# Expert weight tiles laid out and loaded in pairs, one 1 MB transfer for two ring slots

## The reference, cut to what matters

```python
q = jnp.einsum('td,de->te', xt, w_query).reshape(n_tok, PEER_HEADS, 2, HALF_KEY)
sc = jnp.einsum('thpk,hpnk->thpn', q, sub_keys)
va, ia = lax.top_k(sc[:, :, 0], PEER_TOPK)
vb, ib = lax.top_k(sc[:, :, 1], PEER_TOPK)
...
gate = jax.nn.softmax(top, axis=-1)
...
act = _gelu(jnp.einsum('tkd,td->tk', w_down[eb], xb))
return jnp.einsum('tk,tkd->td', gb * act, w_up[eb])
```

## Time and profile before

| | us |
|---|---|
| median of 3 runs | 1558.21 |
| runs | 1556.63, 1558.33, 1558.21 |
| span of the profiled execution (its own time is not printed beside it) | 1555.7 |
| TensorE busy | 1539.2 (99%) |
| VectorE, GpSimd, ScalarE busy | 1129.0, 742.5, 640.0 |
| down stage (first to last of lines 1307 to 1309) | 439.7 to 1021 |
| up stage (lines 1669 to 1671) | 1021.5 to 1544 |

### The profile page before, as it was taken

One profiled execution on the slowest core, in us unless ns is written; L12 is line 12 of the kernel. 1 busy time (PEld: TensorE's weight loads), 2 busy tenths in 40 slices (PEclk: granted clock), 3 DMA queues, 4 the chain that ended last, 5 costly groups with the idle time before them and its releaser, 6 DMA issues.

```text
span 1555.7 us, 23483 instructions
## 1 busy us (share of the span) xinstructions
PE 1539.2 (99%) x8604; PEld 1388.1 (89%) x8604; DVE 1129.0 (73%) x2355; ACT 640.0 (41%) x851; POOL 742.5 (48%) x452
## 2 busy tenths in 40 slices
PE   8999999999999999999999999999999999999997
PEld 8888899888899999999999999988888888888885
DVE  5564262477999877687759763788888888888796
ACT  5323244423234456446644663343333333333333
POOL 1543572224346976777678767732222322323230
PEclk9999999999999999999999999999999999999998
DMA  8532250332245987899799879999999999999991
GB/s 308 188 108 82 95 176 28 108 136 96 81 142 185 352 273 249 318 416 330 244 348 416 303 252 342 375 358 351 346 349 341 354 341 345 346 350 350 372 350 58
DMA packets 141147, 410.84 MB, mean 264 GB/s; under 512 B 15344, under 2 KB 49392, under 8 KB 140528
## 3 DMA queue, kind: packets, MB, share of 16 engines
q1 hardware_dynamic: 97984, 253.86, 46.6%
q0 software_dynamic: 36864, 134.23, 23.3%
q10 hardware_dynamic: 6192, 21.32, 3.5%
HBM read 363.22 MB, written 46.14 MB: 263 GB/s over the span
## 4 chain that ended last, share of the span: by engine, by line
PE 89%; DVE 9%; issue 1%; DMA 0%; POOL 0%; DVEq 0%; SPq 0%; ACT 0%
PE ps L1670 11%; PE ps L1671 11%; PE ps L1669 11%; PE ps L1307 10%; PE ps L1309 10%; PE ps L1308 10%; PE ps L433 6%; PE ps L435 6%; PE ps L434 6%; PE ps L1640 1%; PE ps L1642 1%; DVE gmat L1007 1%; DVE gmat L1000 1%; DVE gmat L1001 1%; DVE gmat L997 1%
## 5 line engine op out<-in xcount | busy, mean ns | idle before, releaser
L1525 ACT ACTIVATE w_hi<-raw 128x1024 fp32r<-128x1024 f32 x252 | 266.6, 1058 | 339.5 <-PE ps L1671 302.9
L1307 PE MATMUL ps<-b_hi,w_hi 128*128 128x384 f32 x1024 | 346.5, 338 | 0.2 <-POOL w_lo L1491 0.2
L1309 PE MATMUL ps<-b_hi,w_lo 128*128 128x384 f32 x1024 | 342.4, 334 | 0.0
L1308 PE MATMUL ps<-b_lo,w_hi 128*128 128x384 f32 x1024 | 342.2, 334 | 0.0
L1491 POOL TENSOR_TENSOR w_lo<-raw,w_hi 128x1024 fp32r<-128x1024 f32 x119 | 286.7, 2410 | 107.6 <-ACT w_hi L1525 106.3
L1499 POOL DMA_INDIRECT rows<-in_w_up,expert x128 | 151.7, 1185 | 341.4 <-DVE ps L1738 329.4
L1671 PE MATMUL ps<-w_hi,b_lo 128*128 128x512 f32 x768 | 298.8, 389 | 0.0
L1670 PE MATMUL ps<-w_lo,b_hi 128*128 128x512 f32 x768 | 298.8, 389 | 0.0
L1669 PE MATMUL ps<-w_hi,b_hi 128*128 128x512 f32 x768 | 298.8, 389 | 0.0
L1704 DVE SCALAR_TENSOR_TENSOR rows<-rows,ps 128x1024 f32<-128x1024 f32 x128 | 155.6, 1219 | 92.8 <-DMA rows<-in_w_down,expert 85.4
L1745 DVE TENSOR_TENSOR w_lo<-raw,w_hi 128x1024 fp32r<-128x1024 f32 x133 | 162.8, 1224 | 69.4 <-ACT w_hi L1525 69.4
(11 more groups left out here) (265 smaller groups left out, 2481.5 us busy)
## 6 DMA issues: line engine op xcount, KB each, us to landing
raw<-in_down_t SPq DMA_DIRECT2D x128, 512.0 KB
raw<-in_up_t SPq DMA_DIRECT2D x128, 512.0 KB
raw<-in_units SPq DMA_DIRECT2D x75, 512.0 KB, 3.4
act_d<-act_t SPq DMA_DIRECT2D x128, 192.0 KB
c<-act_d SPq DMA_DIRECT2D x128, 192.0 KB
gate_d<-gmat ACTq DMA_DIRECT2D x32, 512.0 KB
v<-gate_d SPq DMA_DIRECT2D x16, 512.0 KB
i<-gate_d SPq DMA_DIRECT2D x16, 512.0 KB
```

The source lines that it names most:

```text
L1307: nc.tensor.matmul(out, ring.w_hi[:, s, w], b_hi[:, c, 0:DT], start=c == 0, stop=False)
L1308: nc.tensor.matmul(out, ring.w_hi[:, s, w], b_lo[:, c, 0:DT], start=False, stop=False)
L1309: last = nc.tensor.matmul(out, ring.w_lo[:, s, w], b_hi[:, c, 0:DT], start=False, stop=c == KC - 1)
L1525: nc.scalar.activation(w_hi[:, u % W4, :], raw[:, u % W4, :], ACT.Copy).then_inc(hi_done, 1)
```

## The change

Both weight arrays are laid out so that two consecutive tiles lie side by side in a partition's row of 8 KB. SP loads such a pair with one transfer of 1 MB into two neighbouring slots of the ring. The pair is issued at the odd tiles, once both slots are free. A single semaphore, that of the even slot, tells that a pair has landed. The first eight tiles are still loaded one by one, now as halves of the 8 KB rows.

```diff
-            def load(u):
-                sp.wait_ge(split_done, u - W4 + 1)
-                src = t["down_t"][u] if u < TILES else t["up_t"][u - TILES]
-                sp.dma_start(raw[:, u % W4, :], src).then_inc(raw_full[u % W4], 16)
+            def load_pair(u):
+                s = u % W4
+                sp.wait_ge(split_done, u - W4 + 2)
+                src = t["down_t"][u // 2] if u < TILES else t["up_t"][(u - TILES) // 2]
+                sp.dma_start(raw[:, s:s + 2, :].rearrange("p a n -> p (a n)"), src).then_inc(raw_full[s], 16)
...
                 sp.dma_start(t["act_d"][u], act_t[:, u % ACTS, :]).then_inc(act_stored[u % ACTS], 16)
-                load(u + 2 * W4)
+                if u % 2:
+                    load_pair(u + 2 * W4 - 1)
...
             for j in range(TILES - 2 * W4):
-                load(TILES + j + 2 * W4)
+                if j % 2:
+                    load_pair(TILES + j + 2 * W4 - 1)
                 load_act(j + 2 * W4)
...
             def high_part(u):
-                act.wait_ge(raw_full[u % W4], 16 * (u // W4) + 16)
+                act.wait_ge(raw_full[u % W4 if u < 2 * W4 else u % W4 // 2 * 2], 16 * (u // W4) + 16)
...
-            ("front", ins["units"]), ("query", ins["units"][FRONT_UNITS:]), ("down", ins["down_t"]))]
+            ("front", ins["units"]), ("query", ins["units"][FRONT_UNITS:]),
+            ("down", [ins["down_t"][u // 2, :, u % 2 * D:(u % 2 + 1) * D] for u in range(2 * RING)]))]
...
-        "down_t": c(w_down[0].reshape(NK, NK, KC, P).transpose(1, 3, 2, 0)).reshape(NK, P, D),
-        "up_t": c(w_up[0].reshape(NK, NK, D).transpose(1, 0, 2)),
+        "down_t": c(w_down[0].reshape(NK, NK // 2, 2, KC, P).transpose(1, 4, 2, 3, 0)).reshape(NK // 2, P, 2 * D),
+        "up_t": c(w_up[0].reshape(NK, NK // 2, 2, D).transpose(1, 0, 2, 3)).reshape(NK // 2, P, 2 * D),
```

## The result

The changed kernel takes 1567.21 us (1566.08 to 1569.1, four runs) against 1557.42 us (1556.37 to 1558.33) for the one before on the same chip: 1.0064 times as long, with an interval of 1.0052 to 1.0076, or 9.8 us. The forecast was 4.1 us, and the top of its range is passed by 0.2 us. The profiled execution has a span of 1564.9 us against 1555.7, so 9.2 us of the difference are in the trace. In the file after the change the lines lie one to three further down: the pair's load is L1436, the high part L1528, the Gelu L1534, the gate copy L1545, GpSimd's low part L1494.

The account below looks back on a forecast made before the run. The prediction took TensorE, busy 1539.2 of 1555.7 us, to set the time; 0 + 2.3 + 1.8 = 4.1 us of stalls on the median 1558.2 gave 1562.3 us, range 1556.5 to 1567.

Parts of the forecast that it names:

- the removed issues: SP's queue: 124 of 248 weight loads go, 0.33 us each, on a queue that mostly waits; gain 0.
- a queue already full: First gate stores: loads of tiles 56 and 57 took 16.5 and 16.2 us, read as a backlogged DMA queue.
- the hidden case: Rival: pairs land soon enough everywhere, for instance if 8 KB pieces drain the queue faster; 1558.2 us, chance 0.38.
- The two terms of the stores: TensorE stalls in the first and second gate-store stretches of the down stage: 2.3 us and 1.8 us.
- the turn ahead of tile 89: Second gate stores: TensorE's turn of VectorE's picks, up to 2.6 us late if gathers slow down.
- The first gathers: Tiles 18 and 19: pair has 7.0 us to land, expected between 4.9 and 8.9, middle 6.9; cost 0.
- three places: Down-stage places priced: first gathers 0, first gate stores 2.3, second gate stores 1.8 us.
- The layout: First eight tiles as halves of 8 KB rows, same 4 KB pieces at another pitch: cost 0.
- faster: Rival: TensorE is fed at another rate, with only 4.9 us of waits open; about 1554 us, chance 0.06.
- The gathers or stores paying: Rival: weights win DMA share, so gate stores or gathers come late; about 1561 us, chance 0.12.
- The loop: Rival, up stage: pairs over 10.5 us lengthen rounds; at 11.5 us, 1.0 us in each of 30, 1588 us; chance 0.04.
- the 9.9 that the prediction allowed: Up stage: time for a pair to land before the even tile's high part, 9.9 us instead of 14.0; cost 0.

Follow-up runs that it names:

- e14_bank_gates_before: Kernel before, with a third PSUM bank for down tiles and, in gate-round tiles, gate copies ahead of the next high part on ScalarE; 1559.0 us, ratio 1.0005.
- the second profile: Profile of a repeat measurement of the changed kernel, unaltered, on the same chip; 1565.22 us, ratio 1.005 to the kernel before.
- e1_layout: Kernel before with the 8 KB row layout only, every tile loaded singly as a 4 KB half at its old time; 1558.61 us, ratio 1.0008.
- e4_4kb: Changed kernel with the old layout, a pair still one 1 MB transfer but in 4 KB pieces; 1571.4 us, ratio 1.0087 to the kernel before.
- e8_quiet: Changed kernel with single loads at tiles 16 to 23, 52 to 65, 84 to 97 and 112 to 127; 1560.59 us, ratio 1.0018 to the kernel before.

## Why the prediction was wrong in size

**Right.** The change is slower, for the reason named: TensorE, with next to no waits before, gets waits behind Gelus that stand behind late high parts. The up stage costs next to nothing, although ScalarE does wait there, 28.4 us in nine waits, one of 9.8 us; and nothing is gained by the removed issues (SPq has 0% of the chain that ended last). The stretch of the earlier trace rows, read as a queue already full, still is. ScalarE's waits in the down stage rose above 32.1 us, all of them at even tiles, as the text asked.

The busy rows around the first stores (engines' busy us, granted clock, share, GB/s), first two of the kernel before, then three of the one after:

```profile
670.00:680.00 10.00, 10.00 (x59) 10.00 (x58) 10.00 (x10) 3.11 (x4) 7.64 (x5) 1.00 1.03 416
680.00:690.00 10.00, 10.00 (x59) 10.00 (x59) 8.68 (x13) 4.13 (x6) 5.93 (x5) 1.00 1.03 416
...
660.00:670.00 10.00, 10.00 (x60) 10.00 (x59) 9.69 (x38) 5.06 (x7) 6.67 (x5) 1.00 1.03 419
670.00:680.00 10.00, 10.00 (x60) 10.00 (x59) 9.97 (x11) 4.19 (x6) 6.94 (x6) 1.00 1.02 388
680.00:690.00 10.00, 10.00 (x59) 10.00 (x58) 10.00 (x9) 2.88 (x4) 8.36 (x6) 1.00 1.01 398
```

With pieces twice as large the engines are as busy and move no more: 419, 388 and 398 GB/s where it was 417, 416 and 416. So the full queue did not drain faster, one of the ways in which the hidden case was to come true.

**The two terms of the stores** came out right together by luck: 1.6 and 2.3 us against 2.3 and 1.8, 3.9 against 4.1, in one profile, and 1.2 and 0.8 us in the second. Their working was off. I let the pair of tiles 56 and 57 go out at 670.00 and land at 686.17. It went out 5.5 us later, as the low part that frees its second slot ended only at 675.45, and landed in 9.0 us, not 16.2:

```profile
675.49 0.33 SPq L1436 DMA_DIRECT2D raw<-in_down_t  x1
...
684.53 1.06 ACT L1528 ACTIVATE w_hi<-raw 128x1024 fp32r<-128x1024 f32 x1 [5.11 <-DMA raw<-in_down_t]
```

The two errors nearly cancel, tile 55 lost nothing and tile 57 0.4 us. Tiles 61 and 62 paid behind gate copies, a second thing in the same queue that I had not followed; in the second stores the largest step is at tile 91 (1.3 us), not at 87, and the turn ahead of tile 89, which had raised that term from 1.0 to 1.8, was not late. (It was, by 1.1 us, in the profile of e14_bank_gates_before, which has no pairs.)

**The step that failed first** is "The first gathers ... I take 0". It took the middle between 4.9 and 8.9 us for the landing, 6.9, just under the 7.0 that were allowed. The pair took 8.56 us (502.43 to 510.99) and tile 17 lost 1.7, and 1.5 in the second profile. The nearest row was the one of the same size and form, 1 MB in 8 KB pieces at 8.9 us; a time for half the bytes is only a lower end.

**The step that failed most** is the list itself: the sum has three places because I looked at gathers and gate stores, and left out the last stretch of the down stage. Tile 112 lost 0.9 us, where GpSimd's low part comes late behind gathers, and tile 125 lost 2.4, where the low parts have passed to VectorE and stand behind dots that wait for gathered rows. Before, that place had slack. The Gelu of tile 123 ran from 1005.22 to 1005.71, with nothing in its way but TensorE, 3.5 us ahead of tile 125's start at 1009.18. The pair, issued at 1007.35 and over 9 us on its way, used it up. With these the steps make 1.7 + 1.6 + 2.3 + 0.9 + 2.4 = 8.9 us, of 9.3 (in the second profile 5.7 us, of 6.1 at tile 127). The layout, another term put at nothing, measured 1.3 us in e1_layout, with an interval that allows 0.

**The rivals.** Hidden and faster: the new waits for L1307 exclude both. The gathers or stores paying: the waits for gathered rows rose, the longest from 5.5 to 7.3 us, as that rival said, but not for its reason, as e4_4kb shows; ScalarE was never idle ahead of a gate copy (L1545), so its wait for the stores cost nothing. The loop did not close: after a pair is issued in the up stage it lands in 7.5 us in the median (issue view of the profile after, KB each and median us), under the 9.9 that the prediction allowed; three of the 64 took longer, one 17.1 us while the last inputs were loaded, and none made a loop.

```profile
raw<-in_up_t SPq DMA_DIRECT2D x64, 1024.0 KB, 7.5
raw<-in_down_t SPq DMA_DIRECT2D x60, 1024.0 KB, 7.8
```

**Open.** At tiles 112 and 123 to 125, how much is the pair's landing and how much the gathers that its wait delays was not separated. Nor was it tried to keep pairs and split only those issued within some tiles of a store stretch, apart from e8_quiet, which is still 3.0 us above before. A ring with more slots, in which a pair could be asked for earlier, was not tried either. And why TensorE's clock fell after some waits and not after others stays open. No version here beats the kernel before, and of its waits only 0.2 us lie in the weight stages.

## What to carry to other kernels

Two transfers merged into one give two tiles one landing: the first half waits for the second half's bytes, and if it was asked for early it is now asked for late too. Price that at every place where the first half has little slack, over the whole stage, by the row of the merged size, and follow everything that stands in the in-order queue behind the waiting instruction, not only the first thing. When a fix removes one wait and most of the time stays, read which instruction in the same queue has come up next. And where TensorE falls behind by more than it waited, read its granted clock right after the wait.

## What the runs showed that I had not expected

- The hardware queue of the loads has 17,856 packets fewer (80128 for 97984), and its share of the DMA engines' time went from 46.6% to 46.2% only.
- The merged transfer in 4 KB pieces (1.0087, 1.0071 to 1.0103) comes out 4 to 6 us above the one in 8 KB pieces (1.0064 and 1.005, with intervals that end at 1.0076 and 1.0064, the first of which overlaps). So the larger piece seems to help, only less than the merging costs.
- Moving one ScalarE instruction behind the next tile's Gelu, with no transfer changed, costs the kernel before 14 us, of which some 4.7 are tiles that TensorE ran at its lower clock after a wait.
- ScalarE's 120.9 us of waiting for down weights show up as 5.3 us of TensorE's waits for Gelus, less than one part in twenty; in the second profile 114.7 us show up as 2.1.
